# One core, a two-layer float32 network: the output gate of a gated linear attention goes through seven block products

## The chip, the core and the metric

One core of a Trainium2 chip. The metric is the device time of one execution in microseconds; the time before is the median of three runs. Engines: PE (TensorE) multiplies, ACT (ScalarE) and DVE (VectorE) do the elementwise work, POOL (GpSimd) some more and the accumulating DMAs, SP issues the loads of weights.

## The reference, cut to what matters

The network is a first block (SwiGLU FFN `f1`, a mixer, FFN `f2`, a gated embedding) and two layers of FFN, mixer, FFN (`a0`, GLA, `a1`; `b0`, retention, `b1`), on 256 tokens of width 1024, all in float32. The change lies in the GLA mixer:

```python
q, k, v, r, g_low = split_cols(x @ w_in, GLA_SPLITS)     # 512, 512, 1024, 1024, 16 columns
log_a = jax.nn.log_sigmoid(g_low @ w_gate + b_gate) / GLA_TAU
o = rms_norm_2(gla_chunked(q, k, v, log_a), norm_g)      # 4 heads, chunks of 64 tokens
return (o.reshape(bsz, l, GLA_VAL) * jax.nn.silu(r)) @ w_out
```

`r`, 256 tokens by 1024 columns, is the output gate. `gla_chunked` multiplies queries and keys by exponentials of a running sum of `log_a` within each chunk.

## The kernel before, in words

Every weight tile is 128 partitions by 2048 float32: four blocks of 128 rows by 512 columns. To multiply in nearly full precision, each operand is split in a rounded part and a rest. For a tile, SP loads it into a `whole` block (L599), ACT writes the rounded copy into another block (`split`, L1436), and DVE writes the rest, whole less rounded, over the loaded block (L1876). A pass (`pe_pass`, L814) of 128 tokens is then 12 matmuls: rounded tokens by rounded tile, rests of tokens by rounded tile, rounded tokens by the tile's rest (L833, L837, L846, L850). `pe_columns` does the same with the tile as the stationary side, for queries and keys, whose results are wanted transposed (L929, L931, L932): 48 matmuls a tile.

There are 14 blocks of weights (5 slots of two in the mixers). A planner in Python gives each tile its two blocks, always the one whose last use is oldest. `needed[i]` is the index of the last tile that must have been used before tile i can be loaded and rounded. ACT and DVE each take the tiles in order; where they do so is written out by hand as `act_high(ahead(i))` and `dve_lows(ahead(i))`. `ahead(i, gap=2)` (L521) goes from tile i up to the last tile whose `needed` is at most i - gap. Each engine runs its own instruction list in order and waits on semaphores. A wait holds all that stands behind it on that engine.

The FFNs use a scheme of seven products in place of eight for a pair of their column tiles. Tokens (2 blocks of 128) by input width (2 blocks of 512) times width by columns (2 blocks) would be eight block products. With four sums of the token blocks (`dve_token_sums`, L2109), split like everything else (`sh` on ACT, L1626; `sl` on DVE, L2199), and four sums of the weight blocks, it is seven (`pe_product`, L890): b11, t1, t2, b22, t3, b21, t4. The tiles of t1 and t3 are made by an accumulating DMA (`pool_sum`), those of t2 and t4 by DVE (`dve_weight_sums`, L1883). Results are put together from banks 6 and 7 by an eviction on ACT (u1, s5, u2) and a sum on DVE (c12, c22, c11). The token blocks as they are (not split) are copied from PSUM into `xn` by ACT (`act_tokens`, L1450).

The GLA stage runs from about 740 to 850 us. Order on PE (`pe_gla`, L1193): values `gv` (four tiles, two passes each), the low-rank tokens `gl`, queries' first tile `gq[0]`, then a wait for `glT` (the low-rank tokens copied by DVE into `xn`, L2324), the small product `z` (L1205), `gq[1]`, keys `gk[0]`, `gk[1]`, then the gate's eight passes (four tiles `gr`) with the scores, the scores across chunks and values amid them, then the transposes of the output and its four tiles `go`. ACT and DVE meanwhile make the chain of decay: z with bias (DVE L2330) into `g1`, abs, exp, ln (ACT, `g2`), min and subtract, a scan, a subtraction to the chunk's end (DVE), three exps (ACT L1737, L1738, L1740), then the queries' and keys' products with them (DVE L2346 to L2361). After `o` come squares, a root, the reciprocal (DVE L2377), silu of the gate (ACT L1746), its product with the norm's gain (POOL L733), and the scaling (DVE L2387). `glT`, the gate's small weights `wg` and the masked scores `gsT`, `gsX` lie in `xn` in this stage.

Of the kernel before, what the change touches and what calls it, by code (L numbers as in the profile page):

```python
# [17 lines left out]
P = 128  # L18
# [50 lines left out]
ORDER = {"f1": LATE, "f2": TWO, "a0": TWO, "a1": TWO, "b0": TWO, "b1": TWO}  # L69

# [75 lines left out]
Ffn = namedtuple("Ffn", "name nx turned_raw th tl sx sh sl sg hh")  # L146
Group = namedtuple("Group", "first second b11 t1 t2 b22 t3 b21 t4")
# [3 lines left out]
def build(nc, A, out):  # L151
    with ExitStack() as ctx:
# [75 lines left out]
        with ExitStack() as ar:  # L228
            goh = sb("goh", [P, 8, 256], F32R, ar)
            gol = sb("gol", [P, 8, 256], F32R, ar)  # L230
            g1, g2, g3 = [sb("g" + n, [P, 4, 256], F32, ar) for n in ("t1", "t2", "t3")]
            rst = sb("rst", [P, 4, 4, 64], F32, ar)
            gn = sb("gn", [P, 256], F32, ar)
            tri = sb("tri", [P, P], F32, ar)
            bg = sb("bg", [P, 4], F32, ar)
        for n in (3, 4):
# [84 lines left out]
        ACC_GLA = [[bank[0], bank[1]], [bank[2], bank[3]]]  # L321
        OUT_GLA = [[bank[2], bank[3]], [bank[6], bank[7]]]
# [7 lines left out]
        glT, wg = xn[0:64, 0, 512:768], xn[0:64, 1, 512:1024]  # L330
# [31 lines left out]

        def plan_ffn(name):
# [3 lines left out]
            for step, *what in ORDER[name].steps:  # L367
# [3 lines left out]
                elif step == "product":  # L371
                    g, m = what
                    j = ORDER[name].pairs[g]
                    spot[name, g, m] = i = len(tiles)
                    product_of[i] = (name, g, m)
                    plan(name + "gu", {"b11": gate_up(j, 0), "b21": gate_up(j, 1), "b22": gate_up(j + 1, 1),
                                       "t1": gate_up(j + 1, 0), "t3": gate_up(j + 1, 0)}.get(m), 4)
                    if m in ("t1", "t3"):
                        addend[i] = gate_up(j, 0) if m == "t1" else gate_up(j + 1, 1)
                    if m == "t4":  # L380
                        grp = group[name, g] = Group(j, j + 1, *(spot[name, g, m] for m in Group._fields[2:]))
                        load_key[grp.t1], load_key[grp.t3], load_key[grp.b22], load_key[grp.b21] = (
                            grp.b11 - 0.9, grp.t2 + 0.5, grp.t1 - 0.1, grp.t2 - 0.1)
# [18 lines left out]
        plan_x("gk", w_gla, (1,))  # L402
        plan_x("gr", w_gla, (4, 5))
# [48 lines left out]
        def give_blocks(first, end, among):  # L452

            events = []
            for i in range(first, end):
                if tiles[i].src is not None:
                    events.append((load_key[i] - LOAD_LEAD, "load", i))
                events.append((i - HIGH_LEAD, "high", i))
            for g in group.values():
                if first <= g.b11 < end:  # L460
                    for of, i in ((g.t1, g.t2), (g.t2, g.t4)):
                        events.append((of + 0.6 - HIGH_LEAD, "sum", i))
# [29 lines left out]
        give_slots(at["gv"][0], at["a1gu"][0], range(5))  # L492
# [159 lines left out]
        def pool_program(pool):  # L652
# [116 lines left out]
        def turn_bank(pe, key, by):  # L769

            if len(uses) >= 2:
                old, emptied = uses[-2]
                pe.wait_ge(emptied.sem, emptied.of(*old))
                if old[0] == "x" and old[1] in ORDER and old[1] != "f1":
# [418 lines left out]
        def pe_gla(pe):  # L1193
# [18 lines left out]
            def gate(i, t):  # L1212
                n, k = i // 2, i % 2
                if i == 0 and t == 0:
                    pe.wait_ge(vec.sem, vec.of("z", 3))
                if i == 2 and t == 0:
                    pe.wait_ge(vec.sem, vec.of("qd", 1))
                pe_pass(pe, at["gr"][i], X, 4 * k, t, bank[6 + t] if n == 0 else bank[t], k == 0, k == 1)
# [1421 lines left out]
```

## Time and profile before

| | us |
|---|---|
| median of three runs | 1591.44 |
| lowest, highest | 1590.81, 1591.67 |
| profiled execution | 1591.92 |
| its span | 1590.1 |
| PE busy | 1580.2 (99%), 7659 matmuls |
| DVE busy | 1118.8 (70%) |
| ACT busy | 866.0 (54%) |
| POOL busy | 105.0 (7%) |

The busy shares are means over the whole span. In the stage of the change they are to be read stretch by stretch. Times of rows count from the span's start. In a timeline the first number is the start, the second the duration; instructions of one kind that follow each other are merged and counted with x; a bracket at the end is the idle time before, and what ended it. Instructions that follow each other on one engine overlap a little: their starts lie closer than their durations.

### The profile page before, as it was taken

The page shows a single profiled execution, that of the slowest core. Times are in us where ns is not written, and L with a number is a line of the kernel's source. Part 1 is how long each engine was busy: PE and PEld are TensorE (multiplying, and loading weights), DVE is VectorE, ACT ScalarE, POOL GpSimd, SP SyncE. Part 2 cuts the span into 40 slices and gives each one's busy share as a digit, 9 for nine tenths or more (in the row PEclk, how much of TensorE's full clock was granted, in tenths as well). Part 3 has the DMA queues.
Part 4 walks back from the last instruction along what each step waited for, and adds up shares of the span by engine and source line. Part 5 has one row for each costly group of instructions (what it writes and reads, how often), then busy time and mean ns, then how long its engine had stood idle before and what let it go on. Part 6 is the DMA issues. An engine that isn't in the chain of part 4 may idle for free.

```text
span 1590.1 us, 18691 instructions
## 1 busy us (share of the span) xinstructions
PE 1580.2 (99%) x7659; PEld 1317.9 (83%) x7659; DVE 1118.8 (70%) x1081; ACT 866.0 (54%) x907; POOL 105.0 (7%) x126
## 2 busy tenths in 40 slices
PE   9999999999999999999999999999999999999998
PEld 6888897788888888888988888888888998888886
DVE  6785566677875678865668886678856657688964
ACT  7564457556653766642655665366543435456650
POOL 0141000000000000001010000000000131000000
PEclk9999999999999999999999999999999999999999
DMA  8874463467854687562648765578545544587750
GB/s 339 247 237 190 179 245 133 159 252 231 282 181 172 263 280 265 177 240 96 238 159 310 232 225 213 224 229 287 211 185 196 192 172 152 189 292 233 242 212 27
DMA packets 51892, 341.38 MB, mean 215 GB/s; under 512 B 6240, under 2 KB 6624, under 8 KB 13408
## 3 DMA queue, kind: packets, MB, share of 16 engines
q1 hardware_dynamic: 44000, 301.94, 50.7%
q0 software_dynamic: 7584, 38.12, 10.8%
q8 instruction: 61, 1.00, 0.3%
q14 instruction: 23, 0.19, 0.0%
q10 hardware_dynamic: 224, 0.14, 0.0%
HBM read 339.12 MB, written 1.05 MB: 214 GB/s over the span
## 4 chain that ended last, share of the span: by engine, by line
PE 96%; DVE 2%; DMA 1%; ACT 1%; issue 0%; SPq 0%; DVEq 0%; ACTq 0%
PE bank L833 24%; PE bank L846 24%; PE bank L837 21%; PE bank L895 4%; PE bank L897 4%; PE bank L900 4%; PE bank L783 3%; PE bank L850 3%; PE bank L932 1%; PE bank L931 1%; PE bank L929 1%; DVE split L1876 1%; DMA h<-in_x 0%; DMA whole<-in_w_gla 0%; PE bank L1318 0%; PE bank L1108 0%
## 5 line engine op out<-in xcount | busy, mean ns | idle before, releaser
L1876 DVE TENSOR_TENSOR split<-whole,split 128x2048 fp32r<-128x2048 f32 (+2 forms) x329 | 704.4, 2161 | 203.8 <-ACT split L1436 202.1
L1436 ACT ACTIVATE split<-whole 128x2048 fp32r<-128x2048 f32 (+1 forms) x313 | 581.7, 1876 | 265.2 <-DVE whole L1880 38.7
L833 PE MATMUL bank<-split,xh 128*128 128x512 f32 x1052 | 288.1, 396 | 0.0
L846 PE MATMUL bank<-split,xh 128*128 128x512 f32 x1052 | 282.1, 390 | 0.0
L837 PE MATMUL bank<-split,xl 128*128 128x512 f32 x880 | 235.8, 390 | 0.0
L846 PEld LDWEIGHTS bank<-split,xh 128*128 128x128 f32 x1052 | 197.2, 188 | 41.8 <-DVE split L1876 0.4
L833 PEld LDWEIGHTS bank<-split,xh 128*128 128x128 f32 x1052 | 192.9, 188 | 40.7 <-issue 2.8
L837 PEld LDWEIGHTS bank<-split,xl 128*128 128x128 f32 x880 | 165.2, 188 | 35.4
L833 PE MATMUL bank<-split,th 128*128 128x512 f32 x524 | 143.7, 392 | 0.0
L837 PE MATMUL bank<-split,tl 128*128 128x512 f32 x524 | 142.2, 389 | 0.0
L846 PE MATMUL bank<-split,th 128*128 128x512 f32 x524 | 142.1, 389 | 0.0
L837 PEld LDWEIGHTS bank<-split,tl 128*128 128x128 f32 x524 | 98.4, 188 | 20.7
L846 PEld LDWEIGHTS bank<-split,th 128*128 128x128 f32 x524 | 98.4, 188 | 20.6
L833 PEld LDWEIGHTS bank<-split,th 128*128 128x128 f32 x524 | 97.1, 188 | 19.2
L929 PE MATMUL bank<-xh,split 128*128 128x256 f32 x256 | 72.6, 284 | 0.0
L931 PE MATMUL bank<-xl,split 128*128 128x256 f32 x256 | 72.4, 283 | 0.0
L932 PE MATMUL bank<-xh,split 128*128 128x256 f32 x256 | 72.4, 283 | 0.0
L1441 ACT ACTIVATE th<-bank 128x512 fp32r<-128x512 f32 x66 | 39.3, 597 | 29.1 <-PE bank L783 28.1
L1923 DVE TENSOR_TENSOR tl<-bank,th 128x512 fp32r<-128x512 f32 x66 | 45.3, 688 | 13.5 <-ACT th L1441 13.1
L1880 DVE TENSOR_TENSOR whole<-whole 128x2048 f32<-128x2048 f32 x22 | 50.3, 2284 | 0.0
L929 PEld LDWEIGHTS bank<-xh,split 128*128 128x128 f32 x256 | 49.1, 192 | 0.4 <-issue 0.3
L931 PEld LDWEIGHTS bank<-xl,split 128*128 128x128 f32 x256 | 49.1, 192 | 0.0
(312 smaller groups left out, 1727.0 us busy)
## 6 DMA issues: line engine op xcount, KB each, us to landing
whole<-in_w_a_gate_up SPq DMA_DIRECT2D x48, 1024.0 KB, 7.4
whole<-in_w_b_gate_up SPq DMA_DIRECT2D x48, 1024.0 KB, 7.1
whole<-in_w_f_gate_up SPq DMA_DIRECT2D x45, 1024.0 KB, 7.1
whole<-in_w_ret SPq DMA_DIRECT2D x24, 1024.0 KB, 4.9
whole<-in_w_f_down SPq DMA_DIRECT2D x20, 1024.0 KB, 4.9
whole<-in_w_a_down SPq DMA_DIRECT2D x20, 1024.0 KB, 4.9
whole<-in_w_b_down SPq DMA_DIRECT2D x20, 1024.0 KB, 5.1
whole<-in_w_mix SPq DMA_DIRECT2D x16, 1024.0 KB, 4.9
```

The costliest lines, as they stand in the source:

```text
L833: pe.matmul(o[:, :], tokens(0, k), whi[:, k, :], start=start and k == 0, stop=False, skip_group_check=True)
L837: pe.matmul(o[:, :], tokens(1, k), whi[:, k, :], start=False, stop=False, skip_group_check=True)
L846: ins = pe.matmul(o[:, :], tokens(0, k), wlo[:, k, :], start=False, stop=end, skip_group_check=True)
L895: pe.matmul(o[:, :], xh_of(k), whi[:, k, :], start=start and k == 0, stop=False, skip_group_check=True)
L897: pe.matmul(o[:, :], xl_of(k), whi[:, k, :], start=False, stop=False, skip_group_check=True)
L900: ins = pe.matmul(o[:, :], xh_of(k), wlo[:, k, :], start=False, stop=k == 3, skip_group_check=True)
L929: pe.matmul(o, whi[:, k, cols], xh[:, k0 + k, :], start=start and k == 0 and c % 2 == 0, stop=False, skip_group_check=True)
L931: pe.matmul(o, whi[:, k, cols], xl[:, k0 + k, :], start=False, stop=False, skip_group_check=True)
L932: ins = pe.matmul(o, wlo[:, k, cols], xh[:, k0 + k, :], start=False, stop=end, skip_group_check=True)
L1436: act.activation(split[s][:, 0:n], whole[r][:, 0:n], ACT.Copy).then_inc(hi.mark(i), 1)
L1876: dve.tensor_tensor(split[r][:, c0:c1], whole[r][:, c0:c1], split[s][:, c0:c1].bitcast(F32), ALU.subtract).then_inc(lo.mark(*what), 1)
L1880: dve.tensor_tensor(whole[load_to[i]][:, :], whole[load_to[a]][:, :], whole[load_to[b]][:, :], ALU.add).then_inc(vec.mark("sum", i), 1)
```

## The change

The gate's four tiles and eight passes become one group of seven products. The first column tile pair of the group is (5, 4), the two halves of the gate. b11 stands between keys' two tiles, the rest amid the scores and values. The token sums (`gsx`), their rounded copy (`gsh`) and rest (`gsl`) get a place of their own in the stage's memory, where later the output's blocks `goh`, `gol` and `g1`, `g2` lie; `wg` moves out of `xn` to a place of its own. The tiles from b11 to t4, keys' second among them, get their blocks singly, with leads of 5 and 3 tiles, and no longer in slots of two. PE's waits for banks 4 and 5 now also look at ACT's token copies for `gla`.

```diff
+            with ExitStack() as in1:
+                gsh = sb("gsh", [P, 4, 4, P], F32R, in1)
+                gsl = sb("gsl", [P, 4, 4, P], F32R, in1)
+                gsx = sb("gsx", [P, 4, 4, P], F32, in1)
             goh = sb("goh", [P, 8, 256], F32R, ar)
             gol = sb("gol", [P, 8, 256], F32R, ar)
             g1, g2, g3 = [sb("g" + n, [P, 4, 256], F32, ar) for n in ("t1", "t2", "t3")]
...
-        plan_x("gk", w_gla, (1,))
-        plan_x("gr", w_gla, (4, 5))
+        plan("gk", w_gla[1, 0], 4)
+        for m in ("b11", None, "t1", "t2", "b22", "t3", "b21", "t4"):
+            if m is None:
+                plan("gk", w_gla[1, 1], 4)
+            else:
+                plan_product("gr", "gla", 0, m, lambda c, n: w_gla[c, n], 5, 4)
...
-        give_slots(at["gv"][0], at["a1gu"][0], range(5))
+        give_slots(at["gv"][0], at["gr"][0], range(5))
+        give_blocks(at["gr"][0], at["go"][0], range(10), 5, 3)
+        give_slots(at["go"][0], at["a1gu"][0], range(5))
...
+            pool.wait_ge(vec.sem, vec.of("s", "gla", 3))
             for t in range(2):
...
+            pool_sum(pool, "t1", group["gla", 0].t1)
+            pool_sum(pool, "t3", group["gla", 0].t3)
...
             pe.wait_ge(fn.sem, fn.of("gv", 1, 1))
-            for a in range(2):
-                pe_columns(pe, at["gk"][a], 4 * a, four_out(PAIRS[1]), a == 0, a == 1)
+            pe_columns(pe, at["gk"][0], 0, four_out(PAIRS[1]), True, False)
+            pe.wait_ge(vec.sem, vec.of("z", 3))
+            pe_product(pe, grp.b11, *x_block(0, 0), bank[6], True)
+            pe_columns(pe, at["gk"][1], 4, four_out(PAIRS[1]), False, True)
...
-            gate(0, 0)
-            gate(0, 1)
-            gate(1, 0)
+            pe_product(pe, grp.t1, *s_block(GLA, 0), bank[7], True)
+            pe_product(pe, grp.t2, *s_block(GLA, 1), bank[6], False)
             scores(0)
             scores_across()
-            gate(1, 1)
+            pe_product(pe, grp.b22, *s_block(GLA, 3), bank[7], False)
             scores(1)
-            gate(2, 0)
+            pe_product(pe, grp.t3, *s_block(GLA, 2), bank[6], False)
             values(0)
-            gate(2, 1)
-            gate(3, 0)
-            gate(3, 1)
+            pe.wait_ge(vec.sem, vec.of("c12", "gla", 0))
+            pe_product(pe, grp.b21, *x_block(0, 1), bank[7], True)
+            pe.wait_ge(vec.sem, vec.of("c22", "gla", 0))
+            pe_product(pe, grp.t4, *x_block(1, 1), bank[6], False)
...
             act_lead(act, "gla", at["gv"], unit)
+            act_sums(act, GLA)
             act_high(act, ahead(at["gq"][0]))
...
             act.activation(line(g3), line(g3), ACT.Exp, scale=1.0 / 16).then_inc(fn.mark("ee"), 1)
-            act_high(act, ahead(at["gk"][0]))
-            act_high(act, ahead(at["gk"][1]))
+            act_high(act, ahead(at["gk"][0], 1))
...
+            evict(gu1, bank[6], grp.b11, "u1")
+            act_high(act, ahead(at["gk"][1], 1))
+            evict(gs5, bank[7], grp.t1, "s5")
+            act_high(act, ahead(grp.t1, 1))
+            evict(gu2, bank[6], grp.t2, "u2")
+            act_high(act, ahead(grp.t2, 1))
...
+            act_high(act, ahead(grp.b22, 1))
+            gate_silu(0, 0, "c12")
+            act_high(act, ahead(grp.t3, 1))
+            gate_silu(0, 1, "c22")
             squares(0)
             root(0)
+            act_high(act, ahead(grp.b21, 1))
+            gate_silu(1, 0, "c11")
...
             dve_lead(dve, "gla", at["gv"])
+            dve_token_sums(dve, GLA)
             dve_lows(dve, ahead(at["gl"][0]))
             dve.wait_ge(passed.sem, passed.of(at["gl"][0], 1))
+            dve.wait_ge(vec.sem, vec.of("s", "gla", 3))
             dve.tensor_copy(glT, bank_of.get(("glT",), bank[4])[0:64, 0:256]).then_inc(vec.mark("glT"), 1)
             dve_lows(dve, ahead(at["gq"][0]))
+            dve_sums_low(dve, GLA)
+            dve.wait_ge(vec.sem, vec.of("sl", "gla"))
...
-            dve_lows(dve, ahead(at["gk"][1]))
+            dve_lows(dve, ahead(at["gk"][0], 1))
+            dve_lows(dve, ahead(at["gk"][1], 1))
             dve.wait_ge(passed.sem, passed.of(at["gk"][1], 1))
...
-            dve_lows(dve, ahead(at["gr"][0]))
+            dve_lows(dve, ahead(grp.t1, 1))
...
             masked(0)
+            dve_lows(dve, ahead(grp.t2, 1))
+            dve.tensor_tensor(gu2, bank[7][:, :], gu2, ALU.subtract).then_inc(vec.mark("c12", "gla", 0), 1)
             masked(1)
+            dve_lows(dve, ahead(grp.b22, 1))
+            dve.tensor_tensor(gs5, gs5, bank[6][:, :], ALU.subtract).then_inc(vec.mark("c22", "gla", 0), 1)
+            dve_lows(dve, ahead(grp.t3, 1))
             root(0)
             scaled(0, 0)
+            dve.tensor_tensor(gu1, bank[7][:, :], gu1, ALU.add).then_inc(vec.mark("c11", "gla", 0), 1)
+            dve_lows(dve, ahead(grp.b21, 1))
             scaled(0, 1)
```

In the planner, tile b11 has index three above queries' first tile, keys' second tile four above, then t1, t2, b22, t3, b21, t4. `plan_product` sets the load order of the group as in the FFNs.

## Rows read from the trace of the kernel before

**Rows 1.** PE's waits from 735 to 870 us: who waited for whom, total, times, longest.
```profile
PE bank L1205 <- DVE xn L2324: 0.4, 1, 0.4
PE bank L1228 <- DVE xn L2371: 0.3, 1, 0.3
```

**Rows 2.** One stretch: busy time of PE, PEld, DVE, ACT, POOL, then PEclk, DMA share, GB/s.
```profile
770.00:790.00 20.00, 19.60 (x159) 18.89 (x159) 13.56 (x14) 15.48 (x13) 0.00 (x0) 1.00 0.46 164
```

**Rows 3.** PE's timeline: z, queries' second tile, gate, scores, transposes, output tiles.
```profile
770.73 1.13 PE L1205 MATMUL bank<-xn 32*128 32x256 f32 x8 [0.40 <-DVE xn L2324]
771.79 0.38 PE L929 MATMUL bank<-xh,split 128*128 128x256 f32 x1
...
789.16 1.09 PE L833 MATMUL bank<-split,xh 128*128 128x512 f32 x4
...
791.91 1.07 PE L833 MATMUL bank<-split,xh 128*128 128x512 f32 x4
...
797.44 0.27 PE L1228 MATMUL bank<-gqd,gki 128*64 128x64 f32 x1
...
799.43 1.17 PE L833 MATMUL bank<-split,xh 128*128 128x512 f32 x4
...
816.55 0.60 PE L783 MATMUL bank<-ident,gr 128*128 128x128 f32 x4
...
820.80 1.17 PE L833 MATMUL bank<-split,goh 128*128 128x512 f32 x4
...
829.88 1.16 PE L833 MATMUL bank<-split,goh 128*128 128x512 f32 x4
```

**Rows 4.** DVE's timeline: a rest, glT's copy, z, key products, rests, mask, reciprocal.
```profile
768.06 2.29 DVE L1876 TENSOR_TENSOR split<-whole,split 128x2048 fp32r<-128x2048 f32 x1 [0.82 <-ACT split L1436]
770.26 0.41 DVE L2324 COPY xn<-bank 64x256 f32<-64x256 f32 x1
...
773.21 1.65 DVE L2330 TENSOR_SCALAR gt<-bank,bg 128x256 f32<-128x256 f32 x4
...
793.53 0.69 DVE L2352 TENSOR_TENSOR gki<-bank,gt 128x512 f32<-128x512 f32 x1
...
797.13 4.49 DVE L1876 TENSOR_TENSOR split<-whole,split 128x2048 fp32r<-128x2048 f32 x2
...
802.24 0.43 DVE L2371 TENSOR_TENSOR xn<-bank,tri 64x256 f32<-64x256 f32 x1
...
811.78 0.18 DVE L2377 RECIPROCAL st<-st 128x4 f32<-128x4 f32 x1 [4.40 <-ACT st L1758]
```

**Rows 5.** ACT's timeline: a rounding, abs, the last exp, roundings after it, squares.
```profile
766.11 1.92 ACT L1436 ACTIVATE split<-whole 128x2048 fp32r<-128x2048 f32 x1 [0.72 <-DMA whole<-in_w_gla]
...
774.90 1.06 ACT L1730 ACTIVATE gt<-gt 128x1024 f32<-128x1024 f32 x1 [3.93 <-DVE gt L2330]
...
786.24 1.04 ACT L1740 ACTIVATE gt<-gt 128x1024 f32<-128x1024 f32 x1
787.19 5.51 ACT L1436 ACTIVATE split<-whole 128x2048 fp32r<-128x2048 f32 x3
...
808.57 0.39 ACT L1753 ACTIVATE xn<-bank 128x256 f32<-128x256 f32 x1 [3.71 <-PE bank L1255]
```

**Rows 6.** DVE's timeline in the next FFN: the first and last of four token sums.
```profile
872.38 0.68 DVE L2123 TENSOR_TENSOR sx<-xn 128x512 f32<-128x512 f32 x1
...
874.30 0.69 DVE L2128 TENSOR_TENSOR sx<-xn,sx 128x512 f32<-128x512 f32 x1
```

**Rows 7.** DVE's groups, shapes apart: count, busy us, mean ns, idle before.
```profile
L1880 DVE TENSOR_TENSOR whole<-whole 128x2048 f32<-128x2048 f32 x22 | 50.3, 2284 | 0.0
...
L2199 DVE TENSOR_TENSOR sl<-sx,sh 128x2048 fp32r<-128x2048 f32 x6 | 13.8, 2292 | 18.2 <-ACT sh L1626 18.2
```

**Rows 8.** An accumulating DMA, 730 to 870 us: count, KB, us to landing.
```profile
whole<-in_w_a_gate_up POOLq DMA_DIRECT2D x1, 1024.0 KB, 11.0
```

**Rows 9.** POOL's timeline: one product of the gate with the norm's gain.
```profile
817.42 1.28 POOL L733 TENSOR_TENSOR gr<-gr,gn 128x512 f32<-128x512 f32 x1 [0.39 <-ACT gr L1746]
```

More of the change, by code:

```diff
@@ L320, in build @@
         ACC = [[bank[6], bank[2]], [bank[7], bank[3]]]
-        ACC_GLA = [[bank[0], bank[1]], [bank[2], bank[3]]]
-        OUT_GLA = [[bank[2], bank[3]], [bank[6], bank[7]]]
+        ACC_GLA = [[bank[6], bank[7]], [bank[2], bank[3]]]
+        OUT_GLA = [[bank[2], bank[3]], [bank[0], bank[1]]]
         LAST = bank[0]
@@ L329, in build @@
         diag, ones, factor = xn[:, 0, 512:768], xn[:, 0, 768:896], xn[:, 1, 512:768]
-        glT, wg = xn[0:64, 0, 512:768], xn[0:64, 1, 512:1024]
+        glT = xn[0:64, 0, 512:768]
+        GLA = Sums("gla", gsx, gsh, gsl)
         gsT, gsX = xn[:, :, 0:512], xn[:, 1, 512:1024]
@@ L361, in plan_rows, with plan_product @@
                     plan(key, full[n, c], 4)
+        def plan_product(key, name, g, m, block, first, second):
+            spot[name, g, m] = i = len(tiles)
+            product_of[i] = (name, g, m)
+            plan(key, {"b11": block(first, 0), "b21": block(first, 1), "b22": block(second, 1),
+                       "t1": block(second, 0), "t3": block(second, 0)}.get(m), 4)
+            if m in ("t1", "t3"):
+                addend[i] = block(first, 0) if m == "t1" else block(second, 1)
+            if m == "t4":
+                grp = group[name, g] = Group(first, second, *(spot[name, g, m] for m in Group._fields[2:]))
+                load_key[grp.t1], load_key[grp.t3], load_key[grp.b22], load_key[grp.b21] = (
+                    grp.b11 - 0.9, grp.t2 + 0.5, grp.t1 - 0.1, grp.t2 - 0.1)
         def plan_ffn(name):
@@ L373, in plan_ffn @@
                     j = ORDER[name].pairs[g]
[L374 to L383, printed above, removed]
+                    plan_product(name + "gu", name, g, m, gate_up, j, j + 1)
             plan_rows(name + "d", A[f"w_{name}_down"], A[f"w_{name}_down_head"])
@@ L773, in turn_bank @@
                 pe.wait_ge(emptied.sem, emptied.of(*old))
-                if old[0] == "x" and old[1] in ORDER and old[1] != "f1":
+                if old[0] == "x" and old[1] in RAW_TOKENS:
                     pe.wait_ge(fn.sem, fn.of("xs", *old[1:]))
@@ L1208, in pe_gla @@
             pe.wait_ge(fn.sem, fn.of("gv", 1, 1))
-            for a in range(2):
-                pe_columns(pe, at["gk"][a], 4 * a, four_out(PAIRS[1]), a == 0, a == 1)
[L1212 to L1218, printed above, removed]
+            grp = group["gla", 0]
+            pe_columns(pe, at["gk"][0], 0, four_out(PAIRS[1]), True, False)
+            pe.wait_ge(vec.sem, vec.of("z", 3))
+            pe_product(pe, grp.b11, *x_block(0, 0), bank[6], True)
+            pe_columns(pe, at["gk"][1], 4, four_out(PAIRS[1]), False, True)
             def scores(t):
@@ L1546, in act_lead @@
             act_high(act, ahead(four[1]))
-            if stage in ORDER:
+            if stage in RAW_TOKENS:
                 act_tokens(act, stage, 1)
@@ L1552, in act_lead, with act_sums @@
             act_high(act, ahead(four[3] + 1))
+        def act_sums(act, f):
+            act.wait_ge(vec.sem, vec.of("s", f.name, 3))
+            act.activation(f.sh[:, :, :, :], f.sx[:, :, :, :], ACT.Copy).then_inc(fn.mark("sh", f.name), 1)
         def act_ffn(act, f, e):
@@ L1740, in act_gla, with evict, gate_silu @@
             act.activation(line(g3), line(g3), ACT.Exp, scale=1.0 / 16).then_inc(fn.mark("ee"), 1)
-            act_high(act, ahead(at["gk"][0]))
-            act_high(act, ahead(at["gk"][1]))
-            def gate_silu(n, t):
-                act.wait_ge(passed.sem, passed.of(at["gr"][2 * n + 1], t))
-                act.activation(half(gr[:, t, :], n), (bank[6 + t] if n == 0 else bank[t])[:, :], ACT.Silu).then_inc(
-                    fn.mark("gr", n, t), 1)
+            act_high(act, ahead(at["gk"][0], 1))
+            grp = group["gla", 0]
+            gu1, gu2, gs5 = half(gr[:, 0, :], 1), half(gr[:, 0, :], 0), half(gr[:, 1, :], 0)
+            def evict(dst, src, i, what):
+                act.wait_ge(passed.sem, passed.of(i, 1))
+                act.activation(dst, src[:, :], ACT.Copy).then_inc(fn.mark(what, "gla", 0), 1)
+            def gate_silu(n, t, combined):
+                dst = half(gr[:, t, :], n)
+                act.wait_ge(vec.sem, vec.of(combined, "gla", 0))
+                act.activation(dst, dst, ACT.Silu).then_inc(fn.mark("gr", n, t), 1)
             def squares(t):
```

51 lines of the change are left out of this document (30 added, 21 removed).

## The prediction, made before the changed kernel was run

> **What bounds the kernel now.** Read the waits of TensorE first, around the stage that the change touches: between 735 and 870 us PE stood still twice, 0.4 us for the copy of the low-rank tokens and 0.3 us for the mask of the scores [rows 1]. Nothing else in 135 us held it. The granted clock there is 1.00, the upper of its two levels (2.4 GHz) [rows 2]. So PE's instruction count is the time, a matmul taken away is time won, and every wait that comes instead is time lost. Then read PE's timeline for what each step takes [rows 3], and the timelines of DVE and ACT in the same stretch for how late each of them is [rows 4, 5]. The reader is to see that from 768 to 797 us both follow one another almost without a gap: a weight tile is rounded by ACT, its rest is made by DVE, and between them stands the chain of the decay (abs, exp, ln, log, scan, three exps). PE runs beside that chain on tiles that were split before it. That is the cover on which everything hangs.
>
> **Part 1, the products.** Four tiles of the gate are four times two passes of 12 matmuls. A pass takes 2.72 to 2.75 us (791.91 less 789.16) [rows 3]. Seven products of 12 matmuls stand in their place: -2.72 us. This is the only gain on PE, with the 0.3 us of the second wait, which another wait replaces.
>
> **Part 2, token sums ahead of the low-rank copy.** The rest of keys' first tile begins at 768.06, and glT's copy follows at 770.26 [rows 4]. PE waits for that copy. Now four sums come between, 2.61 us in all (874.30 plus 0.69 less 872.38, the same four in the next FFN) [rows 6], and the copy waits for the last, since it overwrites the tokens that they read. It ends 773.3 and not 770.67; PE's z begins 773.37 in place of 770.73: +2.64 us. The gain is spent here already. The two token copies of t=1 on ACT (0.6 each) fall into its idle stretch before 757 and cost nothing.
>
> **Part 3, the sums' blocks ahead of z.** ACT rounds the sums (as wide as a weight tile, 1.92 us [rows 5]) 772.9 to 774.8; DVE makes the rest (2.29 [rows 7]) to 777.1. Only then may DVE write z, because the raw sums lie on g1 and g2. z took 773.21 to 774.86 [rows 4]; it now ends 778.8. ACT's abs started 774.90 [rows 5] and starts 778.84. The whole chain of decay shifts by 3.94 us: the last exp ended 787.28 and ends 791.2.
>
> **Part 4, where the first block is split.** I worked the planner through. The first product's block b11 takes its rounded copy in a block that queries' first tile frees; `needed` is that tile's index, three below b11. The calls of ACT ahead of and within the chain look back two tiles from queries' first and second tile, so neither reaches b11 (before, the look from queries' second tile took in the gate's first tile, and ACT rounded it between ln and the next exp). So b11 is rounded after the last exp, as the tile at 787.19 was [rows 5]: 791.1 to 793.0. PE is ready for it at 773.37 + 1.06 + two column tiles of 5.79 (789.16 less 771.79, over three) = 786.0. It stands 7.05 us. Queued behind it on PE is everything, keys' second tile too, which needs nothing of it. The 2.64 us of part 2 come ahead of this wait and are paid all the same, since the same sums delay the chain.
> Then DVE: rest of b11 ready 795.3 (wait 0.45 us after eight matmuls, 793.05 + 1.81), rest of keys' second tile 797.5 by the step of 2.2 us in a row of such [rows 4] (PE arrives 796.2, wait 1.3 us). That tile ends 803.35.
>
> **Part 5, DVE from 797.5 on.** Before keys are read out it now makes two weight sums and two rests (2.28 to 2.29 each, step 2.2 [rows 7, 4]): 806.3. Key products and crossings take 3.6 us (793.53 to 797.13) [rows 4]: 809.9. PE does t1, t2, both scores (1.99, 797.44 to 799.43 [rows 3]) to 810.9, nearly unhindered, and b22 to 813.6. DVE goes on with rests of b22 and t3 (4.4), then the mask (1.14, 801.53 to 802.67 [rows 4]): 815.45. Scores of t=1 wait for that bank: 1.9 us. The accumulating DMAs have 11.0 us to landing [rows 8]; t1's is issued about 774, t3's about 786, and they are wanted at 797 and 809: the stall pays for them, nothing added.
> From there PE has 11.4 us of work (799.43 to 816.55 was 17.1, less a product gone, less 0.3 idle, less b22) and stands at the first transpose at 826.9. DVE: two rests to 819.85, c12 to 820.55; ACT: silu 0.6, a rounding of w_gla_out, silu, then squares, table, root (3.21, 808.57 to 811.78) [rows 4, 5]; scaling ends 827.85. Wait 0.95. Transpose, values, transpose take 4.25 (816.55 to 820.80), but the second half's silu stands behind one more rounding and a table load, Pool's product takes 1.28 [rows 9] and scaling 0.88: 832.7, wait 0.9. The output product starts 833.1 where it started 820.80: +12.3. Its third tile is rounded only behind the squares of t=1, 839.0, its rest 841.3, while PE comes at 838.65: 0.35 + 1.35. By 829.88's counterpart [rows 3] the delay is +14.0 us. From there the order is as before, and since PE had no slack later, nothing is given back.
>
> **Sum.** -2.72 - 0.4 (old waits and rounding) + 2.64 + 7.05 + 0.45 + 1.3 + 0.1 + 1.9 + 0.95 + 0.9 + 1.7 = +13.9, +14.0 by the walk. The profiled execution took 1591.92 us (span 1590.1 and 1.8 around it), 0.48 above the median of 1591.44. 1591.92 + 14.0 = 1605.9; against the median 1605.4, I say 1605.5.
> Bounds. Not shown before are POOL's two accumulating loads beside this stage and three more tiles read: cost between 0 (they land 10 us early) and, if one landed as late as twice 11.0, 3 us; I take 0, nearest to the row. SBUF positions alone: 0. The walk's later waits (parts 5) together 5.8 us: from 0, were DVE's and ACT's order kinder than read, to 8.
>
> **The clock.** PE has been at 1.00 in all stretches shown [rows 2] with waits no longer than 0.4 us [rows 1]; after 7 us of standing no row of this trace tells what it does. If the rate of b11 were halved, it costs 2.7 us, and 1.9 + 1.3 + 0.45 us of waiting for DVE stand behind it, so it would be hidden; were keys' second tile (5.8) at half rate too, 8.5 less 3.65 = 4.9 us are left.
> By the Trainium skill, "TensorE: Matmul & The Clock Gate", Part 1, the throttled state is the default and activity releases it, so such a pause would bring the lower clock back. By that rule my time would be between 1605.5 and 1610.4, and it speaks against the change too.
>
> **Rivals.**
> A, the walk: 1605.5, own range 1602 to 1608. For it: each step is one wait between named rows. 0.72.
> B, only the first waits count, the later ones vanish: -2.7 - 0.4 + 2.64 + 7.05 + 1.75 = +8.3, 1599.7. For it: DVE had 4.4 us idle ahead of 811.78 [rows 4], so my order may be pessimistic; against: it has five more 2.2 us steps there. 0.12.
> C, A with the lower clock through b11 and keys' second tile: up to 1610.4. 0.10.
> D, not slower: b11 is rounded in the chain of decay, as the gate's first tile was. Then the chain's shift hits only what PE needs late. Place: ACT at 784.6; price: the 7.05 and most of the rest go, part 2 stays or goes with how early the sums come: 1588.7 to 1591.4. It decides from the point where ACT rounds b11 before 786.0. Against: the index count of part 4. 0.06.
>
> **Chances.** Slower 0.94 (A, B, C), within 0.2% 0.03, faster 0.03 (D split in two); 0.2% or 3 us is what a measurement here can tell. Range for 8 in 10: 1599 to 1610, which takes in B and nearly all of C.
>
> **What would show it.** In the changed kernel: z's matmuls start about 773.4; PE idle about 7 us ahead of the first product, released by ACT's rounding, which stands right behind the third exp; ACT's abs near 778.8; short waits of 1 to 2 us at the scores of t=1, the first transposes and the third output tile; PE's instruction count down by 12. Wrong it would be if ACT rounded a tile between ln and exp, or if the copy of glT came before the token sums.

## The result, and the profile after

| | before | after |
|---|---|---|
| median of the runs, us | 1591.56 | 1607.84 |
| lowest, highest | 1590.81, 1592.09 | 1606.19, 1609.49 |
| profiled execution | 1591.92 | 1609.49 |
| its span | 1590.1 | 1607.7 |
| PE busy | 1580.2 | 1582.8 (12 matmuls fewer) |

The ratio is 1.0102, with a 95% interval of 1.0088 to 1.0116: slower by 16.3 us. The forecast was 1605.5, with a range of 1599 to 1610.

PE has twelve matmuls fewer and is busy 2.6 us longer. Two kinds of line say where the time went. PE's waits over the whole span of the changed kernel (total, times, longest):

```profile
PE bank L915 <- ACT split L1456: 5.4, 1, 5.4
PE bank L1225 <- DVE xn L2365: 3.1, 1, 3.1
PE bank L803 <- DVE gr L2433: 2.2, 2, 1.2
PE bank L803 <- DMA h<-in_x: 2.0, 1, 2.0
PE bank L1243 <- DVE xn L2417: 1.5, 1, 1.5
...
PE bank L866 <- DVE split L1912: 1.1, 1, 1.1
PE bank L880 <- ACT split L1877: 1.0, 1, 1.0
PE bank L1243 <- DVE gkeT L2397: 0.5, 1, 0.5
PE bank L853 <- ACT split L1456: 0.2, 1, 0.2
```

Before, the stage had two waits, 0.7 us together [rows 1]. Now it has eight, 13.9 us together. (The one for `h<-in_x`, the one at L880 and the one left out lie at the kernel's start.) And the granted clock of stretches of the changed kernel (busy time of PE, PEld, DVE, ACT, POOL, then PEclk, DMA share, GB/s):

```profile
10.00:15.00 5.00, 4.28 (x14) 3.47 (x15) 3.48 (x6) 2.35 (x6) 0.00 (x0) 0.66 1.05 429
...
776.00:780.00 4.00, 4.00 (x22) 3.35 (x19) 3.15 (x4) 0.79 (x1) 0.71 (x1) 0.57 1.09 334
780.00:792.00 12.00, 9.77 (x82) 9.57 (x80) 6.06 (x7) 8.77 (x8) 0.86 (x1) 1.00 0.73 175
792.00:796.00 4.00, 0.85 (x2) 0.79 (x3) 1.67 (x3) 4.00 (x4) 0.00 (x0) 0.63 0.89 178
796.00:800.00 4.00, 4.00 (x11) 3.05 (x11) 4.00 (x3) 0.81 (x1) 0.00 (x0) 0.51 0.29 59
```

Before, the clock was 1.00 from 770 to 790 us [rows 2]. Now it falls to its lower level (1.2 GHz) twice: about 776.0, just behind PE's 3.1 us wait (1.00 from 774 to 776, 0.50 from 776 to 778), and about 793.1, within the 5.4 us wait.

One correction must be made ahead of comparing times. The changed kernel's profiled execution is 2.0 us late from its start on: an issue of POOL in the first mixer stands at 198.43 us before and here, in POOL's timeline, at

```profile
200.45 0.58 POOL L654 DMA_DIRECT2D gain<-in_mix_post_g  x1 [58.67 <-DVE st L2000]
```

Its first stretch shows 0.66 (10 to 15 us; before, the same stretch had 1.00), and its wait for `in_x` was 2.0 us, 1.3 before. The four runs of the changed kernel lie in two pairs 3.2 us apart (1606.2 and 1606.3; 1609.4 and 1609.5), and the profiled one is of the later pair. Two kernels of the experiments, `filler` and `early`, show the same 0.66 and a start 1.7 to 1.8 us late, and in both the profiled execution belongs to the slower ones. So it is likely that the two pairs differ by this start, but it was not shown. The change doesn't touch that part, so times of the stage are read here less 2.0.

For the same reason a median of the changed kernel holds two late starts, and a difference of 1 or 2 us against it says little. A stretch of the trace that begins behind the start is the better measure: from PE's transposes of `h` ahead of the stage to those near 1200 us, in the layer behind it (starts of the rows L783 or L803, `bank<-ident,h`):

| | ahead | behind | stretch, us |
|---|---|---|---|
| before | 748.07 | 1203.29 | 455.2 |
| changed | 750.08 | 1220.86 | 470.8 |

By it the change costs 15.6 us; the other 0.7 us between the medians lie outside the stage. Each stretch is of one execution.

PE's timeline of the changed kernel, at the counterparts of [rows 3]:

```profile
775.42 1.55 PE L1225 MATMUL bank<-xn,wg 32*128 32x256 f32 x8 [3.08 <-DVE xn L2365]
...
795.15 2.04 PE L915 MATMUL bank<-split,xh 128*128 128x512 f32 x4 [5.38 <-ACT split L1456]
...
800.18 0.28 PE L949 MATMUL bank<-xh,split 128*128 128x256 f32 x1
...
805.93 1.09 PE L915 MATMUL bank<-split,gsh 128*128 128x512 f32 x4
...
812.05 0.24 PE L1243 MATMUL bank<-gqd,gki 128*64 128x64 f32 x1 [0.49 <-DVE gkeT L2397]
...
818.62 0.27 PE L1243 MATMUL bank<-gqd,gki 128*64 128x64 f32 x1 [1.50 <-DVE xn L2417]
...
831.04 0.66 PE L803 MATMUL bank<-ident,gr 128*128 128x128 f32 x4 [1.16 <-DVE gr L2433]
...
836.15 0.66 PE L803 MATMUL bank<-ident,gr 128*128 128x128 f32 x4 [1.00 <-DVE gr L2433]
...
844.70 1.19 PE L866 MATMUL bank<-split,goh 128*128 128x512 f32 x4 [1.07 <-DVE split L1912]
...
847.44 1.17 PE L853 MATMUL bank<-split,goh 128*128 128x512 f32 x4
```

The last line is the counterpart of 829.88 [rows 3]: +17.56, or +15.6 for the stage. The span grew by 17.6: nothing comes or goes elsewhere. The 15.6 are: the eight waits 13.9, less the two old ones 0.7; the lower clock through z and queries' second tile 1.7 (z and two column tiles took 14.35 us, where 18.43 less 5.79 = 12.64 before); the lower clock through b11 2.3 (5.03 us, where a product takes 2.72); less one product, 2.7. That makes 14.5. The last 1.1 is spread in steps of 0.1 to 0.3 over the products beside waits (t2's took 2.88 us and b22's 2.98, in place of 2.72), and no single row holds it.

ACT and DVE of the changed kernel (their timelines), where the chain of decay and b11's split stand:

```profile
780.84 1.06 ACT L1754 ACTIVATE gt<-gt 128x1024 f32<-128x1024 f32 x1 [4.05 <-DVE gt L2373]
...
792.16 1.04 ACT L1764 ACTIVATE gt<-gt 128x1024 f32<-128x1024 f32 x1
793.11 3.70 ACT L1456 ACTIVATE split<-whole 128x2048 fp32r<-128x2048 f32 x2
```

```profile
776.82 2.29 DVE L2168 TENSOR_TENSOR gsl<-gsx,gsh 128x2048 fp32r<-128x2048 f32 x1 [1.46 <-ACT gsh L1576]
779.14 1.66 DVE L2373 TENSOR_SCALAR gt<-bank,bg 128x256 f32<-128x256 f32 x4
...
802.81 2.29 DVE L1912 TENSOR_TENSOR split<-whole,split 128x2048 fp32r<-128x2048 f32 x1 [1.08 <-ACT split L1456]
```

Abs starts at 780.84, less 2.0 that is 778.84, the time that the prediction gave. b11 is rounded right behind the third exp. Both stood as it said.

### The profile page after: what moved, and what is told of

Same layout as the page of the kernel before. It is cut to its first block, busy times and chain, and to the rows that moved or that the text cites. A ratio compares the mean times of both kernels' runs of the same rounds, so it can differ in the third digit from the quotient of the medians.

```text
span 1607.7 us, 18713 instructions
## 1 busy us (share of the span) xinstructions
PE 1582.8 (98%) x7647; PEld 1318.9 (82%) x7647; DVE 1136.8 (71%) x1094; ACT 876.4 (55%) x918; POOL 108.3 (7%) x128
## 4 chain that ended last, share of the span: by engine, by line
PE 94%; DVE 3%; ACT 2%; DMA 1%; issue 1%; SPq 0%; POOL 0%; DVEq 0%; ACTq 0%
PE bank L853 24%; PE bank L866 24%; PE bank L857 21%; PE bank L915 5%; PE bank L917 4%; PE bank L920 4%; PE bank L803 3%; PE bank L870 3%; PE bank L952 1%; PE bank L951 1%; PE bank L949 1%; DVE split L1912 1%; ACT split L1456 1%; DMA h<-in_x 0%; DMA whole<-in_w_gla 0%
## 5 line engine op out<-in xcount | busy, mean ns | idle before, releaser
L853 PE MATMUL bank<-split,xh 128*128 128x512 f32 x1020 | 279.5, 396 | 0.0
L866 PE MATMUL bank<-split,xh 128*128 128x512 f32 x1020 | 273.5, 390 | 0.0
L857 PE MATMUL bank<-split,xl 128*128 128x512 f32 x848 | 227.2, 390 | 0.0
L866 PEld LDWEIGHTS bank<-split,xh 128*128 128x128 f32 x1020 | 191.2, 188 | 40.5 <-DVE split L1912 0.2
L853 PEld LDWEIGHTS bank<-split,xh 128*128 128x128 f32 x1020 | 187.8, 189 | 39.6 <-issue 2.8
L857 PEld LDWEIGHTS bank<-split,xl 128*128 128x128 f32 x848 | 159.2, 188 | 34.0
L1916 DVE TENSOR_TENSOR whole<-whole 128x2048 f32<-128x2048 f32 x24 | 54.8, 2283 | 0.0
```

What stands on the lines that cost most here:

```text
L853: pe.matmul(o[:, :], tokens(0, k), whi[:, k, :], start=start and k == 0, stop=False, skip_group_check=True)
L857: pe.matmul(o[:, :], tokens(1, k), whi[:, k, :], start=False, stop=False, skip_group_check=True)
L866: ins = pe.matmul(o[:, :], tokens(0, k), wlo[:, k, :], start=False, stop=end, skip_group_check=True)
L1916: dve.tensor_tensor(whole[load_to[i]][:, :], whole[load_to[a]][:, :], whole[load_to[b]][:, :], ALU.add).then_inc(vec.mark("sum", i), 1)
```

## The experiments

Theory: the sums and their rounded pair lie in front of the chain of decay (parts 2 and 3), b11 is rounded only behind that chain (part 4), and in the late part DVE's and ACT's order holds PE (part 5). Rivals: that the place of the copy of `glT` costs by itself (part 2), and that the lower clock is an independent cost. All ratios are against the kernel before on the same chip. In the tables, the stretch is that of the section above, and its difference is taken to the 455.2 us of the kernel before; gains of single steps are told by it.

**1, 2, 3. One part at a time.** `copy_first`: `glT` in g3's place, and its copy ahead of the sums.

```diff
-        glT = xn[0:64, 0, 512:768]
+        glT = g3[0:64, 0, :]
-            dve_token_sums(dve, GLA)
             dve_lows(dve, ahead(at["gl"][0]))
...
             dve.tensor_copy(glT, ...)
+            dve_token_sums(dve, GLA)
```

> The changed kernel, but the low-rank copy glT goes to the place of g3 and is made before the four token sums; everything else as it is. Theory (the chain of token sums, sh, sl, z, decay, rounding of b11 sets the first product, and TensorE's wait for the copy lies beside it): the 3.1 us wait at z goes, the wait at b11 grows from 5.4 by about 3 us or more, and the time stays within 1 us of the changed kernel's 1607.8. Rival (every wait on TensorE is paid by itself): about 3 us less, 1604.7.

`split_in_chain`: b11 is rounded between ln and the next exp.

```diff
-            act_high(act, ahead(at["gq"][1]))
+            act_high(act, ahead(at["gq"][1], 1))
...
-            dve_lows(dve, ahead(at["gq"][1]))
+            dve_lows(dve, ahead(at["gq"][1], 1))
```

> The changed kernel, with b11 rounded by ACT between ln and the next exp and its rest made by DVE behind the last subtraction of the chain. Theory (DVE's row of rests and weight sums behind it is the next bound): b11 starts some 5 us earlier, waits of about 2.2 us for its rest and 2.6 us for the rest of keys' second tile come instead, and about 3.4 us are won: 1604.4. Rival (the whole wait of 5.4 us and the lower clock after it are the cost of this placement): 7 to 8 us less, about 1600.

`sums_in_lead`: sums, rounded copy and rest are made while PE does the values, some 16 us earlier.

```diff
 # ACT, while PE does the values
+            if stage == "gla":
+                act_sums(act, GLA)
             unit(0, 1)
 # DVE, there too; both are gone from where the change has them
+            if stage == "gla":
+                dve_token_sums(dve, GLA)
+                dve_sums_low(dve, GLA)
```

> The changed kernel, with token sums, their rounding and their rest made in the lead, where DVE stands idle for 8 us before queries' first tile arrives; nothing is between that tile's row of rests and z. Theory: z and the chain of decay start as before the change, b11 is rounded 3.9 us earlier, and 3.9 to 4.5 us are won: about 1603.6. TensorE still stands about 6 us ahead of b11. Rival (the sums cost nothing, the wait is another's, such as the load of the tiles): no change, 1607.8.

Measured:

| | median, us | ratio, 95% | stretch, us | PE at z waits | PE at b11 waits |
|---|---|---|---|---|---|
| changed | 1607.84 | 1.0102 [1.0088, 1.0116] | +15.6 | 3.1 | 5.4 |
| copy_first | 1607.76 | 1.0102 [1.0087, 1.0117] | +16.6 | 0.8 | 10.0 |
| split_in_chain | 1605.21 | 1.0084 [1.0067, 1.0100] | +13.9 | 3.2 | 0, but 2.1 and 2.5 for DVE |
| sums_in_lead | 1601.72 | 1.0065 [1.0050, 1.0080] | +10.7 | 0.4 | 4.4 |

In copy_first, PE's timeline:

```profile
770.67 1.13 PE L1225 MATMUL bank<-gt,wg 32*128 32x256 f32 x8 [0.81 <-DVE gt L2363]
...
793.47 2.04 PE L915 MATMUL bank<-split,xh 128*128 128x512 f32 x4 [9.96 <-ACT split L1456]
```

z is back within 0.4 us of its old place in the stage (its wait is 0.8 us, 0.4 before [rows 3]). b11 isn't helped at all: what was saved ahead of it is waited for in front of it. The stretch is even some 1.1 us longer, since the copy now stands ahead of the sums and b11 starts 0.8 us later; the theory's "within 1 us" held by the median and just missed by the stretch. PE's 3.1 us wait at z and the 1.7 us of lower clock behind it thus cost nothing by themselves. They lie in the shadow of the chain that releases b11.

split_in_chain gained 1.7 us (2.6 by the medians) of some 3.4 expected. PE's timeline shows where the rest stays:

```profile
791.45 1.20 PE L920 MATMUL bank<-split,xh 128*128 128x512 f32 x4 [2.14 <-DVE split L1912]
795.11 0.58 PE L949 MATMUL bank<-xh,split 128*128 128x256 f32 x1 [2.46 <-DVE split L1912]
```

The rounding on ACT is no longer late; the rests on DVE are. One releaser took the other's place.

sums_in_lead gained 4.9 us where 3.9 to 4.5 were expected; the medians' 6.1 holds the late starts of the changed kernel. Without the sums DVE writes z at

```profile
771.64 1.66 DVE L2375 TENSOR_SCALAR gt<-bank,bg 128x256 f32<-128x256 f32 x4 [1.29 <-PE bank L1225]
```

and that is 1.2 us earlier in the stage than before the change (773.21, [rows 4], where the stage began 0.4 us later), because a rest of keys that stood ahead of it there has another place in the changed order. The chain and b11 start 5.1 us earlier than in the changed kernel. b11 waits 4.4 us, where about 6 were expected.

**4. Both together.** `both` has the two edits above.

> The two edits together: sums in the lead and b11 split in the chain. Theory: both act on the same path and add, about 7.3 us less than the changed kernel, 1600.5; what is left against the kernel before, some 9 us, are waits for DVE at the rests of b11 and keys' second tile, at scores, and at the transposes. Rival (only the first wait counts): within 1 us of 1591.56 - 2.7 = 1588.9.

1599.82 (1.0051 [1.0036, 1.0066]); expected about 1600.5. The stretch is +8.2. The gains add up nearly: 1.7 + 4.9 = 6.6, measured 7.4, where 7.3 were expected.

**5. The clock by itself.** `filler` puts 24 matmuls on unused data into PE's wait ahead of b11. Bank 7 is free there.

```diff
             pe.wait_ge(vec.sem, vec.of("z", 3))
+            for _ in range(24):
+                pe.matmul(bank[7][:, :], junk[:, 0:P], junk[:, 0:512], start=True, stop=True, ...)
             pe_product(pe, grp.b11, *x_block(0, 0), bank[6], True)
```

> The changed kernel with 24 matmuls of zeros (128x512, bf16, into a bank that nobody reads) put into TensorE's wait ahead of b11, some 5.2 us of work in a wait of 5.4 us. It tells what the lower clock of b11 costs: in the changed kernel b11 took 5.03 us from 795.15 in place of 2.72. Theory (DVE is the bound right behind it, so only what ACT and DVE get later from b11's end is paid): b11's matmuls run at the upper clock, keys' second tile starts when its rest is there, 0.7 us earlier, t1 is rounded 1 us earlier, and 1.1 us are won. Rival (b11's 2.3 us are paid in full): 2.3 us or more won. If the filler outlasts the wait: nothing won.

Granted clock and busy time in the stretch of b11 (0.63 and 0.51 in the changed kernel, above):

```profile
790.00:800.00 10.00, 8.69 (x39) 4.70 (x38) 7.66 (x6) 8.17 (x7) 0.86 (x1) 1.00 0.59 105
```

The clock stays at its upper level there (at z, ahead of the filler, it fell as before). The median is 1607.15 (1.0098 [1.0085, 1.0112]), 0.7 less than the change, which lies within both intervals; the stretch is +14.6, 1.0 less than the change, where the theory had 1.1. PE stands 0.2 and 1.0 us for DVE behind b11, waits that the slow b11 had covered. What is gained comes by another way: b11 ends 1.5 us earlier in the stage, ACT's copy of it and the rounding of t1 follow, and DVE makes t1's rest without the idle 1.08 us that the changed kernel has ahead of it (802.81 above):

```profile
801.40 2.29 DVE L1914 TENSOR_TENSOR split<-whole,split 128x2048 fp32r<-128x2048 f32 x1
```

From there all of DVE's order is 1.0 us earlier. So of the 2.3 us that the lower clock added to b11, 1.0 was paid and 1.2 were hidden by DVE's rests. That is the cover the prediction named, only smaller than it said (3.65).

**6. b11 rounded ahead of the chain.** `early` is `both`, with b11 rounded before abs, its rest made behind z, and keys' second tile split within the chain.

```diff
-            act_high(act, ahead(at["gq"][0]))
+            act_high(act, group["gla", 0].b11)
...
-            act_high(act, ahead(at["gq"][1], 1))
+            act_high(act, at["gk"][1])
 # DVE
+            dve_lows(dve, group["gla", 0].b11)
             dve.wait_ge(fn.sem, fn.of("ln"))
-            dve_lows(dve, ahead(at["gq"][1], 1))
+            dve_lows(dve, at["gk"][1])
```

> Sums in the lead as before, and now b11 is rounded ahead of abs and its rest made while DVE waits for ln; keys' second tile takes b11's place in the chain of decay. Theory: the waits of 1.2 us at b11's rest and 2.5 us at keys' second tile shrink to about 0.5 us together, DVE's row of rests behind qd begins one tile (2.2 us) earlier, and 2.2 to 3.5 us are won against 'both' (1599.8): about 1597. Rival (the later waits, at scores and the transposes, hold the time by themselves): no change from 1599.8.

1596.98 (1.0035 [1.0021, 1.0049]); the stretch is +4.8, some 3.3 less than `both`, where 2.2 to 3.5 were expected. b11 has no wait now (PE's timeline):

```profile
785.64 1.09 PE L915 MATMUL bank<-split,xh 128*128 128x512 f32 x4
```

What is left is mostly the later waits (1.5 and 1.0 at the scores, 2.1 at the transposes, 1.1 at the third output tile): part 5 by itself.

**7, 8, 9. The late part.** `reordered`: on PE the first scores stand ahead of t2; ACT rounds t2, t3, t4 and the output's tiles earlier, with the squares between the silus; DVE makes t3, b21 and t4's rests in that order, and c12, c22, c11 as soon as their banks are full.

```diff
-            pe_product(pe, grp.t2, *s_block(GLA, 1), bank[6], False)
             scores(0)
             scores_across()
+            pe_product(pe, grp.t2, *s_block(GLA, 1), bank[6], False)
...
-            dve_lows(dve, ahead(at["gk"][0], 1))
-            dve_lows(dve, ahead(at["gk"][1], 1))
+            dve_lows(dve, group["gla", 0].t1)
```

> 'early' with DVE's work in the order in which TensorE needs it: keys are read out before t2's weight sum and rest, the scores before t2 on TensorE, the mask before later rests, the combinations as soon as their products are there, squares ahead of the second silu, output tiles rounded and their rests made singly. Theory: the waits at the mask (0.4), the transposes (2.1) and the output tiles (1.3) mostly go, one weight sum still holds t4 or b21 for some 2 us; about 4 us less than 'early', 1592 to 1594. Rival (DVE has too much work whatever its order): within 1.5 us of 'early'.

`reordered_pool`: the weights' sum of t4 is made by POOL.

```diff
+            pool.tensor_tensor(whole[load_to[g.t4]][:, :], whole[load_to[g.b21]][:, :], whole[load_to[g.t2]][:, :],
+                               ALU.add).then_inc(gp.mark("sum", g.t4), 1)
```

> 'reordered' with the weight sum of t4 made by POOL, idle at that time, in place of DVE. Theory: DVE is relieved of 2.2 us in its fullest stretch, no product waits, and the gain of one product is left: 1588 to 1590, faster than the kernel before. Rival (POOL's sum of 128x2048 takes so long, or slows DVE, that t2's rest, which overwrites what it reads, waits for it): 1593 or more.

`final`: that, with three moves.

```diff
             scores(0)
-            scores_across()
             pe_product(pe, grp.t2, *s_block(GLA, 1), bank[6], False)
...
             pe_product(pe, grp.b22, *s_block(GLA, 3), bank[7], False)
+            scores_across()
             scores(1)
```

> reordered_pool with three more moves: scores_across stands behind b22's four matmuls instead of ahead of them, b22's rest is rounded before kx and qx, and go's first rounded tile comes after both silus. Theory (the stage is a chain DVE, PE, ACT whose order decides, and 1.3 us of waits of TensorE at L1261 behind gqx and the turn's 0.7 are still in it): about 1.6 us less than reordered_pool's 1591.5, so 1589.9, 0.999 of the kernel before. Rival (what is left on the chain lies on VectorE, and the moves only exchange one wait for another): 1591.5, no change. Second rival (b22's rest pushes kx and qx back, and the scores of tile 1 with them): 1592.5.

| | median, us | ratio, 95% | stretch, us | PE's waits, 735 to 870 us |
|---|---|---|---|---|
| reordered | 1591.78 | 1.0003 [0.9993, 1.0012] | +0.1 | 2.7 |
| reordered_pool | 1591.51 | 1.0001 [0.9992, 1.0009] | -0.4 | 2.4 |
| final | 1590.09 | 0.9993 [0.9984, 1.0002] | -1.3 | 1.1 |

reordered takes 4.8 us off `early` (5.2 by the medians), a little more than expected: the late waits were the order of ACT and DVE, as part 5 said, and not the work itself. reordered_pool missed its 1588 to 1590. VectorE lost a sum of 2.28 us and got part of it back as waiting. DVE's timeline of reordered, without POOL's sum:

```profile
795.25 0.42 DVE L2403 TENSOR_TENSOR gkx<-gkeT,gt 128x256 f32<-128x256 f32 x1
```

and of reordered_pool, first DVE, then POOL:

```profile
789.76 2.28 DVE L1921 TENSOR_TENSOR split<-whole,split 128x2048 fp32r<-128x2048 f32 x1
792.56 0.69 DVE L2408 TENSOR_TENSOR gki<-bank,gt 128x512 f32<-128x512 f32 x1 [0.52 <-PE bank L958]
...
795.08 1.72 DVE L2413 TENSOR_TENSOR gkx<-gkeT,gt 128x256 f32<-128x256 f32 x1
```

```profile
790.01 6.50 POOL L752 TENSOR_TENSOR whole<-whole 128x2048 f32<-128x2048 f32 x1 [1.72 <-DVE whole L1925]
```

The operation at 795.08 ends at 796.80, 0.3 us behind POOL's end at 796.51, where it otherwise takes 0.42. And PE waits for what follows it: 1.3 us at L1261, the wait that final's moves took away. final's waits (the stage, whole list):

```profile
PE bank L926 <- DVE split L1921: 0.5, 1, 0.5
PE bank L1231 <- DVE xn L2378: 0.4, 1, 0.4
PE bank L955 <- DVE split L1921: 0.2, 1, 0.2
```

final came within 0.2 us of the 1589.9 that it was given. Its interval takes in 1, so it cannot be told from the kernel before. Its median lies 1.07 us under that of the kernel before (1591.16 in that comparison); the product less on PE would be 2.7.

**10. The sums alone.** `sums_only` is the kernel before with the token sums and their rounded pair at the change's places, and no block product.

> The kernel before with the change's token sums alone: the sums of h^T, their copy and their rounded pair stand on VectorE where the change has them, g3's block product is kept in its old form and nothing consumes the sums. It leaves out the seven-product form, and so its wait. Theory (the sums cost their place on VectorE: z 2.6 to 3.1 us later; the rounded pair's 3.9 us in front of it delays abs and the gate's softplus, while TensorE has g3's products to do meanwhile): about +3 us, 1594.5. Rival (most of the change's 16 us comes with the sums and their place, and the new product order adds little): 1602 or more. Second rival (the sums are hidden beside TensorE's work): 1591.5.

1599.67 (1.0053 [1.0040, 1.0065]): +8.5 us, and +7.8 by the stretch. All three expectations missed: it lies between the theory's 1594.5 and the rival's 1602 or more. PE's waits in the stage:

```profile
PE bank L1214 <- DVE xn L2345: 2.9, 1, 2.9
PE bank L1237 <- DVE xn L2394: 1.5, 1, 1.5
PE bank L1237 <- DVE gkeT L2376: 1.0, 1, 1.0
```

and PE's timeline behind the first of them:

```profile
773.20 2.08 PE L1214 MATMUL bank<-xn,wg 32*128 32x256 f32 x8 [2.91 <-DVE xn L2345]
775.20 0.58 PE L938 MATMUL bank<-xh,split 128*128 128x256 f32 x1
...
779.83 0.28 PE L938 MATMUL bank<-xh,split 128*128 128x256 f32 x1
779.95 0.28 PE L940 MATMUL bank<-xl,split 128*128 128x256 f32 x1
```

The wait is 2.9 us, 2.5 more than before. z's eight matmuls take 2.00 us to the next start in place of 1.06 [rows 3], and the following 21 matmuls take 4.63 us, where at the spacing of the last two rows (0.12) they would take 2.5: the lower clock costs 3.0 us here. The scores wait 2.5 us in place of 0.3. Together 2.5 + 3.0 + 2.2 = 7.7; the span grew by 7.8. But that list tells where PE spent the time, and not what set it. DVE's timeline does, with z and the first product of keys:

```profile
780.93 1.66 DVE L2353 TENSOR_SCALAR gt<-bank,bg 128x256 f32<-128x256 f32 x4
...
801.26 0.68 DVE L2375 TENSOR_TENSOR gki<-bank,gt 128x512 f32<-128x512 f32 x1
```

Both stand 7.7 us behind their old places (773.21 and 793.53, [rows 4]), and none of the idle times of DVE and ACT from 772 us to the scores names PE. The scores wait for the products of this row (`gkeT`, above). So the chain's delay makes up the 7.8 us. With the clock at its upper level PE would have come to the scores 3 us earlier and, as the rows stand, waited 3 us longer; no run here tested that apart. My expectation had the chain 3.9 us later and hidden beside PE's work. It was 7.7, since here a rest of keys (776.40) stands between the sums and z too, which the changed kernel makes elsewhere. For that reason the 7.8 us are no share of the change's 15.6.

## Why the prediction was right

The time came out 2.3 us above the forecast, within the range, on the side of rival C. 1.6 of it are a miss of the walk in the stage (+15.6 where it had +14.0), and 0.7 lie outside the stage. Steps against the trace, less 2.0:

| step | predicted | measured |
|---|---|---|
| z starts | 773.37 | 773.42 |
| abs starts | 778.84 | 778.84 |
| PE ready for b11 | 786.0 | 787.77 |
| b11 starts | 793.05 | 793.15 |
| keys' second tile starts | 797.5 | 798.18 |
| it ends, t1 starts | 803.35 | 803.93 |
| crossings ready (DVE) | 809.9 | 811.1 |
| first scores start | 808.9 | 810.05 |
| wait at the scores of t=1 | 1.9 | 1.5 |
| wait at the first transposes | 0.95 | 1.16 |
| wait at the second | 0.9 | 1.00 |
| waits in the third output tile | 0.35 + 1.35 | 0.18 + 1.07 |
| counterpart of 829.88 | +14.0 | +15.6 |

Parts 1, 2 and 3 held to 0.1 us. copy_first shows that the wait of part 2 has no price of its own: without it the sums still delay the chain, as the prediction said.

Part 4 held in its mechanism: the index count, the place behind the third exp, the time. Rival D, b11 rounded within the chain, was made by hand in split_in_chain, and its promise of 1588.7 to 1591.4 was wrong: 1605.2. Even with the sums out of the way (`both`) it gave 1599.8. What D left out is DVE, whose rests of b11 and of keys' second tile come next in the same order.

Where the sum was off is the term of the clock, which it took as nothing. The row said 1.00 with waits up to 0.4 us, and the prediction gave a fall to the lower level a place only behind the 7 us wait. It came also behind the 3.1 us wait at z. There it cost 1.7 us on PE, and this took 1.7 off the 7.05 us wait (5.38 measured), so nothing in time. At b11 it cost 2.3 us; the prediction had 3.65 us of cover for it, and it proved to be 1.2, so that 1.0 was paid: filler, without the slow clock, has waits of 0.2 and 1.0 for DVE where the prediction had 0.45, 1.3 and 1.9. The third, for the mask, could not serve as cover: ACT's eviction of u1 waits for b11's end, the rounding of t1 stands behind it, and DVE's rest of t1 behind that (1.08 us idle ahead of 802.81). So the delay of b11 goes down the chain that sets this wait, and it was 1.5 with the filler too.

The 1.6 us thus fall in two. The gki products start 1.1 us later than predicted, which is DVE's idle time ahead of 802.81, and filler takes 1.0 of it away: that is the clock. The rest comes in small steps behind it, 1.2 at the first transposes (829.04, where the forecast had 827.85), 1.5 at the output product, 1.6 at the counterpart of 829.88. These steps were not tested apart.

Rival B fell: every later wait was there, 5.4 us together. The prediction gave 5.8 for the waits of part 5, but its own terms add up to 5.55. early against reordered shows that most of it can be had back by the order (4.8 us). Rival C was right in its kind, but with 1.0 us in place of 4.9, since keys' second tile ran at the upper level again (5.75 us).

What was taken as nothing, three more loads and two accumulating DMAs beside the stage, cost nothing that shows: no wait of PE in the stage names a DMA, and none of ACT or DVE from 772 to 850 us.

## What to carry to other kernels

An exchange that saves an engine 2.7 us of work by sums and roundings on two others can pay only if those have their time slots ahead of the critical chain, not within it: here the saved product was worth 2.7 us and its preparation, where it stood, cost 18. Walk the order of each in-order engine, and count for each wait who is late next, since undoing one wait (split_in_chain) gave 1.7 where the wait was 5.4, and undoing another (copy_first) gave nothing at all. Look at how an execution starts before a median of four is used for a difference of 1 or 2 us. With the whole order rewritten in five steps (`both`, `early`, `reordered`, `reordered_pool`, `final`), the change comes to level with the kernel before, and not clearly below it.

## What the runs showed of the hardware that was not expected

TensorE's clock fell to its lower level behind waits much shorter than 7 us. Behind 3.1 us (the changed kernel) and 2.9 us (sums_only), part of z and of the tile after it ran at the lower level (to 779.4 from about 776.0, and to 779.8 from z's start at 773.20); behind two waits of 1.2 and 2.5 us close together (`both`) the stretch of 790 to 800 us shows

```profile
790.00:800.00 10.00, 9.76 (x56) 9.46 (x57) 10.00 (x7) 2.13 (x2) 0.00 (x0) 0.74 0.41 85
```

whereas a single wait of 0.8 us (copy_first) left it at 1.00 around z, and the waits of 1.0 to 1.5 us of the changed kernel behind 810 us left it at 1.00 too. So a wait of some 3 us can bring PE about as much again in slow matmuls: 2.9 us of standing brought 3.0 us in sums_only. Whether that is paid is another matter: of the three losses counted here (1.7 and 2.3 in the changed kernel, 3.0 in sums_only) only 1.0 us of the 2.3 went into the time, as far as the rows and `filler` tell. The Trainium skill, "TensorE: Matmul & The Clock Gate", Part 1, says that the throttled state is the default and activity releases it; by that the trace agrees, with 0.57 and 0.51 after the two waits.

VectorE and GpSimd can hold each other up. Above, VectorE's product of two operands in SBUF took 1.72 us in place of 0.42 and ended just behind POOL's sum, while its products with one operand from PSUM (gki, 0.69 us) ran at full speed beside it. POOL's sum, 6.50 us long, starts 0.25 us behind a rest of VectorE, another operation with two operands in SBUF, which ends at 792.04. If POOL could not read before that end, 4.5 us are left for the sum itself, three and a half times the 1.28 us of a quarter as wide an operation [rows 9]. final shows it again, in the timelines of DVE and then of POOL:

```profile
806.74 3.15 DVE L1921 TENSOR_TENSOR split<-whole,split 128x2048 fp32r<-128x2048 f32 x1
```

```profile
806.47 1.28 POOL L759 TENSOR_TENSOR gr<-gr,gn 128x512 f32<-128x512 f32 x1 [10.51 <-ACT gr L1785]
```

The rest takes 3.15 us in place of 2.29, and 806.47 + 1.28 less 806.74 is 1.0. The Trainium skill, "SBUF — State Buffer", in the section "SBUF: two separate sides", describes the pair of ports that the two share as an exclusive lock for the whole instruction, against VectorE's operations with two SBUF inputs; these rows agree. Spans on POOL are rough, and no run here varied its width, so the 4.5 us are an inference.
